# Outputs with blocks as rows and spreads of 128 rows in a state-space stage, and three smaller edits, on one Trainium2 core

## The reference

```python
# _ssd_mixer: 8 heads of 64, 2 groups of 4 heads
seg = a_cs[:, :, :, None] - a_cs[:, :, None, :]
decay = jnp.exp(jnp.where(causal, seg, -jnp.inf))
cb = jnp.einsum('bclgn,bcsgn->bclsg', cm, bm)
y_diag = jnp.einsum('bclsg,bclsgj,bcsgjp->bclgjp', cb, decay, xdt)
...
y = y_diag + y_off + d_skip.astype(f32).reshape(SSD_GROUPS, SSD_HPG, 1) * xs
y = y.reshape(bsz, s, SSD_INNER) * jax.nn.silu(z.astype(f32))
yg = y.reshape(bsz, s, SSD_GROUPS, SSD_INNER // SSD_GROUPS)
yg = yg * lax.rsqrt(jnp.mean(yg * yg, axis=-1, keepdims=True) + EPS)

# _s5_mixer: 32 groups of 16 channels, a complex diagonal state of 64 per group
_, _, h_re, h_im = lax.associative_scan(_complex_affine_combine, (dec_re, dec_im, drive_re, drive_im), axis=0)
y = (jnp.einsum('gip,sbgp->bsgi', c_re.astype(f32), h_re)
     - jnp.einsum('gip,sbgp->bsgi', c_im.astype(f32), h_im) + d_skip.astype(f32) * uf)
gate = jax.nn.gelu(y) @ w_glu.astype(f32) + b_glu.astype(f32)
return (y * jax.nn.sigmoid(gate)).astype(u.dtype)

# hybrid_mixer: three groups of 8 heads, windows and dilations (128, 1), (512, 4), (2048, 16)
q = apply_rotary(qkv[:, :, g, 0], cos, sin)      # x1*cos - x2*sin, x2*cos + x1*sin
k = apply_rotary(qkv[:, :, g, 1], cos, sin)
o, lse = dilated_window_attention(q, k, qkv[:, :, g, 2], window, dilation)
```

## Time and profile before

| | us |
|---|---|
| median of 3 runs | 2978.79 |
| lowest and highest run | 2972.84, 2979.21 |
| the profiled execution, its own time | 2975.73 |
| span of its trace | 2973.9 |
| busy: TensorE | 2810.5 (95%) |
| busy: VectorE | 1459.1 (49%) |
| busy: ScalarE | 949.5 (32%) |
| busy: GpSimd | 202.2 (7%) |
| mean granted TensorE clock | 0.971 |

### The profile page before, as it was taken

The page is one execution under the profiler, slowest core; times in us unless marked ns, Lnnn a source line. Parts: engine busy times, 40 slices in busy tenths (PEclk is TensorE's granted clock), DMA queues, the critical chain, the costliest instruction groups (busy, mean ns, idle before and its releaser), DMA issues. The chain is left out here.

```text
span 2973.9 us, 34050 instructions
## 1 busy us (share of the span) xinstructions
PE 2810.5 (95%) x12640; PEld 2245.9 (76%) x12640; DVE 1459.1 (49%) x1894; ACT 949.5 (32%) x1287; POOL 202.2 (7%) x209
## 2 busy tenths in 40 slices
PE   6999999969999999999988999999999999699997
PEld 5788777547888878888766788887777677488885
DVE  5566347655444344443475544423887335433323
ACT  4432223233333233322234333222224442333212
POOL 3000114101000000000210000000000000000000
PEclk9999999779999999999999999999999999799998
DMA  3344325223333222332311233333441133133321
GB/s 120 113 124 135 126 97 161 62 85 93 99 99 104 94 83 94 99 106 92 110 50 43 92 99 96 114 104 110 135 124 44 43 99 99 47 95 99 106 96 38
DMA packets 82457, 284.69 MB, mean 96 GB/s; under 512 B 14753, under 2 KB 15393, under 8 KB 81473
## 3 DMA queue, kind: packets, MB, share of 16 engines
q1 hardware_dynamic: 71424, 250.54, 26.7%
q0 software_dynamic: 6336, 26.70, 2.8%
q10 hardware_dynamic: 4608, 6.30, 0.9%
HBM read 262.26 MB, written 14.94 MB: 93 GB/s over the span
## 5 line engine op out<-in xcount | busy, mean ns | idle before, releaser
L177 DVE TENSOR_TENSOR wl<-raw,wh 128x1024 fp32r<-128x1024 f32 (+2 forms) x440 | 574.2, 1306 | 1062.7 <-ACT wh L171 1051.8
L223 PE MATMUL PS<-Hh,wl 128*128 128x512 f32 x2232 | 879.7, 394 | 44.2 <-DVE wl L177 20.5
L224 PE MATMUL PS<-Hh,wh 128*128 128x512 f32 x2232 | 872.5, 391 | 0.0
L225 PE MATMUL PS<-Hl,wh 128*128 128x512 f32 x2232 | 872.4, 391 | 0.0
L171 ACT ACTIVATE wh<-raw 128x1024 fp32r<-128x1024 f32 (+2 forms) x440 | 480.1, 1091 | 1145.3 <-PE PS L225 975.5
L223 PEld LDWEIGHTS PS<-Hh,wl 128*128 128x128 f32 x2232 | 421.3, 189 | 148.8 <-issue 51.7
L225 PEld LDWEIGHTS PS<-Hl,wh 128*128 128x128 f32 x2232 | 421.1, 189 | 88.8
L224 PEld LDWEIGHTS PS<-Hh,wh 128*128 128x128 f32 x2232 | 421.5, 189 | 87.8 <-issue 1.5
L225 PE MATMUL PS<-ffn_gl,wh 128*128 128x512 f32 x880 | 350.5, 398 | 0.0
L223 PE MATMUL PS<-ffn_gh,wl 128*128 128x512 f32 x880 | 346.1, 393 | 2.8 <-DVE wl L177 2.8
L224 PE MATMUL PS<-ffn_gh,wh 128*128 128x512 f32 x880 | 348.2, 396 | 0.0
(11 more groups left out here) (409 smaller groups left out, 2599.1 us busy)
## 6 DMA issues: line engine op xcount, KB each, us to landing
raw<-in_gu SPq DMA_DIRECT2D x220, 512.0 KB, 3.6
raw<-in_dn SPq DMA_DIRECT2D x80, 704.0 KB, 4.1
raw<-in_hin SPq DMA_DIRECT2D x44, 512.0 KB, 4.3
raw<-in_oin SPq DMA_DIRECT2D x16, 512.0 KB, 3.7
raw<-in_hin_gate SPq DMA_DIRECT2D x16, 512.0 KB, 3.6
X<-QKV ACTq DMA_DIRECT2D x96, 64.0 KB, 3.2
kept_x<-X POOLq DMA_DIRECT2D x16, 256.0 KB, 3.6
raw<-in_eout SPq DMA_DIRECT2D x8, 512.0 KB, 3.7
```

The source lines that it names most:

```text
L177: self.nc.vector.tensor_sub(self.wl[j % SPLIT][:, 0:kw], self.raw[j][:, 0:kw], self.wh[j % SPLIT][:, 0:kw].bitcast(F32)).then_inc(self.lo_ ...
L223: self.nc.tensor.matmul(out, wl, xh[:, u.k0 + k, :], start=first, stop=False)
L224: self.nc.tensor.matmul(out, wh, xh[:, u.k0 + k, :], start=False, stop=False)
L225: done = self.nc.tensor.matmul(out, wh, xl[:, u.k0 + k, :], start=False, stop=last)
```

## The change

In `states_and_heads` the outputs take the block data as weights (64 columns) and the tables as moving operand (128 columns), two groups at a time in the two halves of the output rows. They now stand ahead of `heads`, wait on `added` instead of `evicted`, and `turn_outputs`, 16 small matmuls with the identity, turns the blocks back into columns. `add_input` reads PSUM. The trip over DRAM is gone. `AT` has 128 rows, zero but for 8, and `spread_a` uses all of them. VectorE's segments are the diagonal blocks alone; ScalarE takes the rest from PSUM with the negated column as bias:

```diff
-OFF = [0, 512, 896, 1152]
+OFF = [512, 896, 1152]
...
                 if q >= 1:
-                    pe.wait_ge(evicted, q)
-                for g in range(8 * q, 8 * q + 8):
-                    out = co.PS[:, 3, NB * (g % 8):NB * (g % 8) + NB]
-                    mm(out, TOE[:, :, g::S5G].rearrange("p l i -> p (l i)"), U8[:, g, :], start=True, stop=False)
-                    m = mm(out, OUT[:, g, :], SB[:, q % 2, g % 8, 0:NB], start=False, stop=True)
+                    pe.wait_ge(added, q)
+                for j in range(4):
+                    out = lambda s: co.PS[NB * s:NB * s + NB, 3, j * P:(j + 1) * P]
+                    for s in range(2):
+                        g = 8 * q + 4 * s + j
+                        mm(out(s), U8[:, g, :], TOE[:, :, 16 * g:16 * g + 16], start=True, stop=False)
+                    for s in range(2):
+                        g = 8 * q + 4 * s + j
+                        m = mm(out(s), SB[:, q % 2, g % 8, 0:NB], OUT[:, g, :], start=False, stop=True)
                 m.then_inc(out_done, 1)
+
+            def turn_outputs(q):
+                pe.wait_ge(evicted, q + 1)
+                for l in range(BL):
+                    for s in range(2):
+                        p = NB * s
+                        m = mm(co.PS[p:p + NB, 3, NB * l:NB * l + NB], YB(q)[p:p + NB, NB * l:NB * l + NB],
+                               co.ident[p:p + NB, p:p + NB], start=True, stop=True)
+                m.then_inc(out_turned, 1)
 
             def spread_a(h):
                 if h >= 2:
-                    pe.wait_ge(seg_ready, h - 1)
-                mm(co.PS[:, 4 + h % 2, :], co.ident[0:SSD_H, h:h + 1].broadcast_to([SSD_H, P]), AT[:], start=True,
+                    pe.wait_ge(lower, h - 1)
+                mm(co.PS[:, 4 + h % 2, :], co.ident[:, h:h + 1].broadcast_to([P, P]), AT[:], start=True,
...
                 if q >= 1:
+                    outputs(q - 1)
                     heads(q - 1)
-                    outputs(q - 1)
+                    turn_outputs(q - 1)
                 swap_states(q)
             outputs(3)
             heads(3)
+            turn_outputs(3)
...
+            def square(c):
+                act.wait_ge(gated, c + 1)
+                act.wait_ge(out_done, c + 1)
+                nc.scalar.activation(SQ[:, c, :], XC[:, c, :], ACT.Square).then_inc(squared, 1)
 
             def power(h):
                 act.wait_ge(seg_ready, h + 1)
-                nc.scalar.activation(SEG[:, h % 3, :], SEG[:, h % 3, :], ACT.Exp).then_inc(powered, 1)
+                for t in range(TT - 1):
+                    m = nc.scalar.activation(SEG[:, h % 3, OFF[t]:OFF[t] + S - (t + 1) * P],
+                                             co.PS[:, 4 + h % 2, (t + 1) * P:], ACT.Exp,
+                                             bias=AC[:, 64 + 8 * t + h:65 + 8 * t + h])
+                m.then_inc(lower, 1)
+                nc.scalar.activation(SEG[:, h % 3, 0:S], SEG[:, h % 3, 0:S], ACT.Exp).then_inc(powered, 1)
...
-                    s = v.tensor_scalar(SEG[:, h % 3, OFF[t]:OFF[t] + S - t * P], co.PS[:, 4 + h % 2, t * P:],
+                    s = v.tensor_scalar(SEG[:, h % 3, t * P:(t + 1) * P], co.PS[:, 4 + h % 2, t * P:(t + 1) * P],
...
             def add_input(q):
-                dve.wait_ge(restored, 16 * (q + 1))
+                dve.wait_ge(out_turned, q + 1)
                 dve.wait_ge(gated, q + 1)
...
                 if q >= 1:
                     skip(q - 1)
-                if q >= 2:
-                    add_input(q - 2)
-            add_input(2)
+                    add_input(q - 1)
             skip(3)
+            add_input(3)
```

In `finish_halves` the sums come before the first unit; only the fourth square is still made there, as the gelu and the other squares moved to the stage ahead:

```diff
-            co.multiply(pe, st, bank_free, chunk_ready=g_parted, between=sums)
+            pe.wait_ge(squared, 1)
+            for c in range(4):
+                m = nc.tensor.matmul(co.PS[:, 4 + c // 2, :], co.ones[:], SQ[:, c, :], start=c % 2 == 0, stop=c % 2 == 1)
+            m.then_inc(summed, 1)
+            co.multiply(pe, st, bank_free, chunk_ready=g_parted)
```

In `hybrid_input` the four transfers of chunk n are issued one unit later, and the sum of `rotate` is written by residue for the dilated groups; `window_attend` reads those contiguously:

```diff
                     if n == 0:
                         act.wait_ge(gated, RAW)
+                    else:
+                        swap(n - 1)
                     co.wait_units(act, st, i, c)
                     nc.scalar.activation(one(QKV, n), one(co.PS, c), ACT.Copy).then_inc(taken, 1)
                     act.wait_ge(taken, n + 1)
                     act.sem_inc(bank_free, 1)
-                    if i > first_qk:
-                        act.wait_ge(done, RAW * (i - first_qk - 1) + c + 1)
-                    for q in range(4):
-                        p, o = 32 * q, 32 * (q ^ 1)
-                        act.dma_start(B[p:p + 32, c], QKV[o:o + 32, n:n + 1, :]).then_inc(swapped[c], 16)
...
-                nc.vector.tensor_add(one(QKV, n), A[c % 2], B[:, c]).then_inc(done, 1)
+                to = one(QKV, n) if n < 8 else QKV[:, n, :].rearrange("p (r q) -> p q r", r=4)
+                by = (lambda t: t) if n < 8 else (lambda t: t.rearrange("p o (q r) -> p (o q) r", r=4))
+                nc.vector.tensor_add(to, by(A[c % 2]), by(B[:, c])).then_inc(done, 1)
...
-                        m = mm(co.PS[:, 2 * (k % 2) + s, (1 + g) * P:(2 + g) * P], QKV[p:p + HD, 8 * g + c, r::4],
-                               QKV[p:p + HD, 8 * g + 4 + c, r::4], start=True, stop=True)
+                        m = mm(co.PS[:, 2 * (k % 2) + s, (1 + g) * P:(2 + g) * P], QKV[p:p + HD, 8 * g + c, r * P:(r + 1) * P],
+                               QKV[p:p + HD, 8 * g + 4 + c, r * P:(r + 1) * P], start=True, stop=True)
```

More of the change, by code:

```diff
@@ L839, in series @@
         g.memset(self.co.ones8[:], 1.0).then_inc(self.filled, 1)
+        g.memset(self.AT, 0.0).then_inc(self.filled, 1)
         pool.wait_ge(self.ready, 8)
@@ L890, in columns @@
                 pe.wait_ge(sizes.ready, SIZE_STEPS)
-                for k, src in enumerate((AT, DT)):
+                for k, src in enumerate((AT[0:SSD_H, :], DT)):
                     for t in range(TT):
@@ L1365, in states_and_heads @@
         (cleared, zeroed, arrived, decayed, driven, copied, swapped, first, turned, scanned, swapped_back, backed, out_done,
-         evicted, own, spread, seg_ready, powered, weighted, y_done, skipped, gated, restored, added, gelued) = (
+         evicted, out_turned, squared, own, spread, seg_ready, lower, powered, weighted, y_done, skipped, gated, added, gelued) = (
             co.sem(f"sh_{s}") for s in (
                 "cleared", "zeroed", "arrived", "decayed", "driven", "copied", "swapped", "first", "turned", "scanned",
-                "swapped_back", "backed", "out_done", "evicted", "own", "spread", "seg_ready", "powered", "weighted",
-                "y_done", "skipped", "gated", "restored", "added", "gelued"))
+                "swapped_back", "backed", "out_done", "evicted", "out_turned", "squared", "own", "spread", "seg_ready", "lower", "powered", "weighted",
+                "y_done", "skipped", "gated", "added", "gelued"))
         block = ctx.enter_context(nc.Block())
@@ L1444, in heads @@
                         h = 2 * c + s
-                        m = mm(co.PS[HD * s:HD * s + HD, 6 + c % 2, t * P:], XDT[:, t, h * HD:(h + 1) * HD],
-                               SEG[:, h % 3, OFF[t]:OFF[t] + S - t * P], start=t == 0, stop=t == TT - 1)
+                        m = mm(co.PS[HD * s:HD * s + HD, 6 + c % 2, t * P:(t + 1) * P], XDT[:, t, h * HD:(h + 1) * HD],
+                               SEG[:, h % 3, t * P:(t + 1) * P], start=t == 0, stop=t == TT - 1)
+                    if t == TT - 1:
+                        break
+                    for s in range(2):
+                        h = 2 * c + s
+                        mm(co.PS[HD * s:HD * s + HD, 6 + c % 2, (t + 1) * P:], XDT[:, t, h * HD:(h + 1) * HD],
+                           SEG[:, h % 3, OFF[t]:OFF[t] + S - (t + 1) * P], start=False, stop=False)
                 m.then_inc(y_done, 1)
@@ L1492, in _ @@
                 power(2 * q + 1)
+                if q >= 2:
+                    square(q - 2)
             evict(3)
-            for c in range(3):
+            square(2)
+            for c in range(4):
                 act.wait_ge(added, c + 1)
@@ L1555, in add_input @@
             def add_input(q):
-                dve.wait_ge(restored, 16 * (q + 1))
+                dve.wait_ge(out_turned, q + 1)
                 dve.wait_ge(gated, q + 1)
-                through(co, v, U, YL, Z, q, cols).then_inc(added, 1)
+                k = cols["s5_d"] + q
+                v.scalar_tensor_tensor(Z[:, q, :].rearrange("p (b l) -> p l b", l=BL), U[:, q], co.cols[:, k:k + 1],
+                                       co.PS[:, 3, :].rearrange("p (l b) -> p l b", b=NB), ALU.mult,
+                                       ALU.add).then_inc(added, 1)
             for q in range(4):
@@ L1613, in _ @@
         def _(pe):
-            def sums(n):
-                if n == 0:
-                    for c in range(4):
-                        pe.wait_ge(squared, c + 1)
```

(28 more changed lines are left out.)

85 lines of the change are left out of this document (35 added, 50 removed).

## The result

The changed kernel takes 2939.45 us (median of 4 runs, 2937.42 to 2941.50) against 2977.53 us before (4 runs): a ratio of 0.9875, 95% interval 0.9858 to 0.9892. Forecast were 2943 us, in a range of 2929 to 2964. The profiled execution took 2941.50 us with a span of 2939.7, 34.2 us less span than before.

The account below looks back on a forecast made before the run. The prediction took most of the kernel as weight-fed matrix work, TensorE busy in 95%, untouched by the change. Four stages gave -16 - 4 - 6.5 - 6 = -32.5 on 2975.7, so 2943 us, range 2929 to 2964.

Parts of the forecast that it names:

- Clock: states_and_heads: spreads over 128 rows instead of 8 raise TensorE's granted clock early, from 0.50 to 1.00.
- 1.00 from the second turn on: states_and_heads: the granted clock expected at 1.00 from the second turn of the loop over q.
- Rival (a): states_and_heads: rows do not matter to the clock, 0.50 for two turns, stage end near 607, total 2950; chance 0.15.
- TensorE's terms: states_and_heads, per turn at clock 1.00: outputs 1.84 us instead of 5.3, turn_outputs 1.3, whole turn 11.4 instead of 13.6.
- rival (e): states_and_heads: output column pairs do not run side by side, clock 0.50, turns of 25.4 us, total 2983; chance 0.05.
- VectorE's turn: states_and_heads: smaller segment pieces save 1.6 us per turn, 14.3 to 12.7 us; VectorE stays the pacer at high clock.
- The tail: states_and_heads: serial end after VectorE's turns at 589.3, with outputs and heads 3.5 us each; end at 600, stage -16.
- finish_halves: Sums ahead of the first glu unit start the norm chain about 6.5 us into the stage instead of 10.65: -4 us.
- hybrid_input: Swap transfers issued behind the split bring query and key units from 5.79 to 5.44 us, 8.0 us lost before: -6.5.
- I take -6.5 (bounds -8 and 0): hybrid_input: the size taken for moving the swap transfers, with the strided write of rotate's sum on VectorE against it.
- window_attend: Contiguous operands for the dilated scores save 0.6 us in each of sixteen steps, at most 10; taken -6, between -1 and -8.
- So **-6: window_attend: of at most 10 us, 6 taken, since in every second step the saving comes back as waiting for ScalarE.

Follow-up runs that it names:

- run 1: The kernel before with AT of 128 rows and the spread over all of them, nothing else of the change: 2970.30 us, against 2975.70 for the kernel before.
- run 2: The changed kernel with the spreads over 8 rows again: 2944.61 us, 5.2 more than the changed kernel.
- Run 9: The changed kernel with all segment differences on VectorE again, and CB and heads in four pieces as before: 2944.54 us, 5.1 more.
- Run 3: The changed kernel with heads ahead of outputs in every turn and at the end: 2937.07 us, 2.4 less.
- run 10: The changed kernel with the sums of squares behind the first glu unit again: 2942.66 us, 3.2 more.
- run 5: The changed kernel with a chunk's four swap transfers issued right behind its eviction again, ahead of the next weight's split: 2947.71 us, 8.3 more.
- Run 4: The changed kernel with ScalarE's copies ahead of the exponentials in window_attend: 2928.92 us, 10.5 less.
- Run 7: The changed kernel with rotate's sum in token order, dilated scores reading every fourth token, and ScalarE's copies ahead of the exponentials in window_attend: 2934.18 us.

## Why the prediction held, point by point

**Clock.** The early rise is right, and runs 1 and 2 show from both sides that the rows make it. "1.00 from the second turn on" was a little too much: the second turn has the fall at 553 (0.83 in 550 to 560). Rival (a), that only busy time counts, falls: 19.06 of 20.00 us busy at 0.50 in run 2, 14.59 of 20.00 in the changed kernel at 1.00 and 0.83. The rule that I cited for it from the Trainium skill ("TensorE: Matmul & The Clock Gate", Part 1) does not agree with these windows if "busy" is read as the busy time of the profile.

**TensorE's terms.** Outputs 1.84 us forecast, 1.77 measured; their turn 1.3 and 1.08. The column pairs do run side by side: the 2048 columns take 1.77 us, while one spread of 512 columns takes 0.92 (561.43 to 562.35), which would make 3.7 one after the other. So rival (e) had no start: its turns of 25.4 us were 9.7, 15.5 and 12.1.

**VectorE's turn.** 12.7 us forecast, 12.8 measured. Run 9 shows the 1.6 us per turn where nothing waits; its stage is 6.1 us longer, of which these turns are not the whole.

**The tail.** End forecast at 600, measured 600.12, from two errors that cancel. The 2 us of waits that I allowed were 3.5, 3.10 us of them at one place I had not named, so VectorE came to the end at 591.1 and not at 589.3: outputs(0) went ahead of heads(0), and with it the load of the table came into heads' way. The wait for `added` was longer than the 4 us I gave it, 6.53, but the clock was back up by the fourth pair of outputs, at 593.9, so that heads(3) took 2.3 us and not 3.5. That gave the 1.8 us back. Run 3 takes out the first and part of the second, 2.1 us.

**finish_halves.** -4 forecast, -4.4 measured. The place of the sums is 4.0 us of it (run 10), the rest is what no longer stands before them.

**hybrid_input.** Direction and mechanism right (run 5), the size 2.7 us too small. The step "I take -6.5 (bounds -8 and 0)" held 1.5 us back for late landings; they became shorter instead, 2.0 for 3.1. And it looked at the query and key units alone: the value units gave another 1.1 us. In them TensorE waited for the low part of a weight 0.67 us at 2199.94 and 0.93 at 2212.04 before, and 0.76 at 2181.86 after, which is 0.8 of it. The prediction also had the fourth transfer issued 3.8 us after the eviction starts, behind a split of 1.1; it is about 2.8, for the issues begin 0.8 us after the eviction does (2045.98 against 2045.19) and run beside the split. The strided write, with steps of 512 bytes, cost 1.10 us a piece, as its nearest row with 16-byte steps had it (1.09), and no time: VectorE is busy 4.9 us of a unit, as worked out.

**window_attend.** Here a term was mis-sized by half: -6 forecast, -3.1 measured. The step that failed is "So **-6**", which let more than half of the 0.6 us per step through. From 2264.53 on, two steps of four gained 0.54 to 0.59 us and two nothing, 1.18 us for four steps (16.54 and 15.36). Over the stage the first four steps gained 0.5 us, the next four 1.8, the next four 1.2 and the three after them 0.6. The end gave 0.9 back, for the clock was at its lower level there (a turn takes 1.83 us at 2300.49 and 1.17 before). The closing chain was named, but not taken as the hard stop that it is. Run 4 shows what it was: the copies behind the exponentials on ScalarE. Run 7 shows that the 0.6 per step itself was right.

**Total.** -32.5 forecast and -32.6 measured over the four stages. That they agree so closely is luck: hybrid_input gave 2.7 us more than forecast and window_attend 2.9 less, and within states_and_heads two errors of 1.8 us cancel. The remaining 1.6 us of the span lie where no edit was made and where the forecast had 0; no run says why.

## What to carry to other kernels

Where TensorE is busy all the time at the lower clock, look at how many of its 128 rows the work uses: padding a small contraction to 128 rows cost no time here (2.02 us a spread against 2.07) and was worth 5 to 9 us, with the old outputs behind it and with the new ones; the clock stayed up afterwards only with both edits. Before pricing a faster piece of work in a software pipeline, write down the loop that closes a step and see on which engine something ready waits behind something not yet needed; exchanging two blocks of ScalarE's order gave 10 us in a stage where halving the time of TensorE's dilated scores gave 3. And when an operation is moved ahead, list what it waits for: it brings its waits with it.

## What the runs showed of the hardware beyond what was expected

A transfer's time from issue to landing depends on the moment of its issue against other traffic: the same 64 KB landed after 3.1 us (before), 3.3 (run 5) and 2.0 (the changed kernel), and the weight loads beside it after 4.6, 4.5 and 3.6. In the changed kernel the clock stayed at 1.00 through the gaps of 1.41 and 1.54 us of each later turn; it was not at 1.00 any more after the gap of 6.53 us, where a group of two outputs took 0.43 us from start to start instead of 0.22. The length of the last gap alone does not tell the two apart: after one of 3.39 us (run 1, before 545.38) the clock was still high, and after one of 2.13 us (the changed kernel, before 551.92) it fell within 1.5 us. What decides between them is open.
